# A two-layer streaming encoder step: the norms' squares added on VectorE, an empty memory left out, and the memory's closing spread over eight banks and two queues

## The chip, the cores and the metric

The kernel runs on one core of a Trainium2 chip. Its time is the device time of the whole program in microseconds (us). The core has five engines that run at once: TensorE (PE, matrix products into the PSUM memory, which has eight banks), VectorE (DVE), ScalarE (ACT), GpSimd (POOL) and SyncE (SP, which starts transfers). Each has its own list of instructions and they meet through semaphores alone.

## What is computed

One inference step of a trunk of two layers, for a prompt of 1024 frames and for 8 running streams of 16 frames. Each layer is a token mixer (layer 0 a diagonal state space with a gated output, layer 1 an mLSTM with a matrix memory) and then a convolutional gated MLP, with an RMS norm before and after every sub-layer. Cut to what matters here:

```
def rms_norm(x, g):
    return x * rsqrt(mean(x * x) + eps) * g

out = ag[..., :D_MODEL] * sigmoid(ag[..., D_MODEL:])        # layer 0's gated output, ag = z @ w_glu
x = x + rms_norm(mix, g[1]); f = conv_ffn(rms_norm(x, g[2]))

# mLSTM, per chunk of the prompt and per head, memory C starts at zero
num = (q k^T * wts) v + a * (q C^T)
den = sum(q k^T * wts) + a * (q n)
C   = decay * C + (wg * v)^T k                                # C and n of the last chunk are outputs
```

## The kernel before

The 1152 frames (1024 of the prompt, 128 of the streams) are the columns of everything; D_MODEL lies in 8 tiles of 128 rows. Columns go in three blocks of 384.

**The gated projection with the first norms.** `front` runs 24 steps (3 blocks of columns by 8 tiles `m`). A step is two weight tiles, each 24 products on TensorE (`products`, L1686). A weight tile is loaded by SP, rounded by ScalarE (`Weights.round`, L836), its remainder is taken by VectorE (`Weights.subtract`, L840), and TensorE waits for both. There are two rooms for weights: a load waits until the remainder of the tile before in its room is taken, and rounding waits until TensorE has used that tile. From the second block on the norms of the block before are put between the steps. `norm1` (class `Norm`) has six groups `g`: for each block the norm of the mixer's output (`r` = 0) and that of the new residual (`r` = 1). A group has four squares of 128x768 (ScalarE, L1526, into three rooms `sq`), their sums over rows and tiles as products with a matrix of ones (TensorE, `sums`, L1536, into bank 6), a root (ScalarE), an inverse (VectorE), its spread to all rows (TensorE, L1560, bank 7) and the scaling (VectorE, L1589). Groups 0 to 3 lie inside the 24 steps: squares at `m` = 0 and 4, sums at `m` = 1 and 5. Groups 4 and 5 come after. GpSimd moves residuals between SBUF and DRAM and takes the remainders `x_rest` (L1565). The order on every engine is written out by hand.

**The prompt cell.** `mlstm_prompt` goes over 8 chunks of 128 frames by 4 heads: two chunks unrolled, a loop, two unrolled. For a head TensorE makes the numerators in one bank pair: the scores by the values (`sc` by `v`, L2797) and then the queries by the memory `ct` (L2799, 4 tiles by 2 halves, added onto the same bank). It then projects the next head (L2666 to L2670), makes the key products (L2813) with the next scores between, and turns the output (L2821). VectorE forms the denominators (L2915 on), the normed row, four memory updates (L2937) and the gain. The third key product waits for the first update. GpSimd has cleared the memory before the first chunk.

**The closing.** A block of its own after the cell. TensorE turns the memory's 16 blocks by the key weights, 4 products each, into banks 0 to 3 in turn (L2966). ScalarE copies each to one of 8 rooms (L2981), SP stores it, 256 KB (L2990). Then the four rows of `n` go through banks 4 to 7 (L2971, L2984, L2993). SP waits for all stores, then a barrier, and `mlstm_down` begins with its weight loads and a clearing of `f`.

## Time and profile before

| | us |
|---|---|
| three runs | 3810.05, 3814.1, 3818.66 |
| median | 3814.1 |
| profiled execution, its time | 3816.18 |
| its span, first to last instruction | 3814.2 |
| TensorE busy in it | 3430.0 (90%) |
| VectorE, ScalarE, GpSimd busy | 1939.5 (51%), 1119.3 (29%), 482.8 (13%) |
| mean granted clock of TensorE | 0.943 of full speed |

A row of the timeline gives start, duration, engine, line, what is written from what, and in brackets how long the engine had been idle and whose work ended that. One product of 32-bit numbers stands as two records. Matmuls overlap, so the distance between two starts is what one costs. Rows of DMA queues name the engine that started the transfer with a q behind it.

### The profile page before, as it was taken

What the parts mean: (1) busy time and instruction counts of PE and PEld (TensorE: products, weight loads), DVE (VectorE), ACT (ScalarE), POOL (GpSimd) and SP (SyncE); (2) the same over time, 40 slices, a digit from 0 to 9 for tenths busy, and PEclk for the clock granted to TensorE, in tenths of its full rate; (3) what the DMA queues carried; (4) which work ended last, traced back from release to release, by engine and by line L of the source; (5) the groups of instructions that cost most, each with busy time, mean ns of one, the idle gap of its engine ahead of it and who ended that gap; (6) DMA issues with size and microseconds to landing.
All of it is one profiled execution on the core that took longest, in us unless ns stands there. A gap on an engine that the chain in (4) does not pass through costs nothing. (4 is left out here: it accounts for less than half of the span.)

```text
span 3814.2 us, 54162 instructions
## 1 busy us (share of the span) xinstructions
PE 3430.0 (90%) x20489; PEld 3239.3 (85%) x20489; DVE 1939.5 (51%) x2954; ACT 1119.3 (29%) x1816; POOL 482.8 (13%) x721
## 2 busy tenths in 40 slices
PE   5549999999999999999759799979959999999997
PEld 4439989999999998999546688879959999999996
DVE  7933455444544464222434466646554555555555
ACT  5233343233223333222223122221133222232221
POOL 2240111010001021000110322310001000000000
PEclk7669999999999999999879899989979999999998
DMA  3445431111111133223256322221033344344433
GB/s 80 133 128 139 130 103 45 45 40 45 43 41 40 45 111 106 105 102 108 57 203 257 89 78 77 78 72 39 31 115 118 123 131 131 116 128 128 127 115 109
DMA packets 357406, 372.72 MB, mean 98 GB/s; under 512 B 42696, under 2 KB 293832, under 8 KB 357060
## 3 DMA queue, kind: packets, MB, share of 16 engines
q1 hardware_dynamic: 340262, 330.43, 27.7%
q0 software_dynamic: 9760, 31.95, 2.7%
q10 hardware_dynamic: 7176, 7.35, 0.6%
q8 instruction: 157, 2.57, 0.3%
q14 instruction: 51, 0.42, 0.0%
HBM read 264.68 MB, written 102.63 MB: 96 GB/s over the span
## 5 line engine op out<-in xcount | busy, mean ns | idle before, releaser
L1686 PE MATMUL pair<-x_head,w_head 128*128 128x384 f32 x1488 | 505.1, 339 | 52.3 <-DVE w_rest L840 28.4
L1686 PE MATMUL pair<-x_rest,w_head 128*128 128x384 f32 x1488 | 501.6, 337 | 0.0
L1686 PE MATMUL pair<-x_head,w_rest 128*128 128x384 f32 x1488 | 501.5, 337 | 0.0
L840 DVE TENSOR_TENSOR w_rest<-w_raw,w_head 128x1024 fp32r<-128x1024 f32 x228 | 291.5, 1279 | 412.8 <-ACT w_head L836 412.7
L836 ACT ACTIVATE w_head<-w_raw 128x1024 fp32r<-128x1024 f32 x228 | 242.2, 1062 | 690.5 <-PE pair L856 167.1
L1336 PE MATMUL pair<-x_head,w_head 128*128 128x384 f32 x1056 | 358.4, 339 | 8.7 <-DVE w_rest L840 7.4
L1336 PE MATMUL pair<-x_head,w_rest 128*128 128x384 f32 x1056 | 353.8, 335 | 0.0
L1336 PE MATMUL pair<-x_rest,w_head 128*128 128x384 f32 x1056 | 353.7, 335 | 0.0
L1686 PEld LDWEIGHTS pair<-x_head,w_head 128*128 128x128 f32 x1488 | 283.1, 190 | 57.5 <-issue 48.2
L1429 DVE SCALAR_TENSOR_TENSOR cv<-u,par,cv 128x1024 f32<-128x1024 f32 x88 | 112.8, 1282 | 341.8 <-ACT u L1395 341.8
L1954 DVE SCALAR_TENSOR_TENSOR cv<-u,par,cv 128x1024 f32<-128x1024 f32 x88 | 112.8, 1281 | 340.9 <-ACT u L1895 340.9
L1686 PEld LDWEIGHTS pair<-x_rest,w_head 128*128 128x128 f32 x1488 | 283.1, 190 | 0.0
L1686 PEld LDWEIGHTS pair<-x_head,w_rest 128*128 128x128 f32 x1488 | 282.6, 190 | 0.0
L1336 PEld LDWEIGHTS pair<-x_head,w_head 128*128 128x128 f32 x1056 | 198.7, 188 | 24.5 <-issue 20.2
L1336 PEld LDWEIGHTS pair<-x_rest,w_head 128*128 128x128 f32 x1056 | 198.8, 188 | 0.0
L1336 PEld LDWEIGHTS pair<-x_head,w_rest 128*128 128x128 f32 x1056 | 198.8, 188 | 0.0
L1390 ACT ACTIVATE cv<-pair,par 128x384 f32<-128x384 f32 x132 | 88.5, 670 | 335.9 <-PE pair L1336 335.9
L1358 PE MATMUL pair<-a_head,w_head 128*128 128x384 f32 x528 | 180.8, 342 | 1.7 <-DVE f L1457 1.5
L1856 PE MATMUL pair<-a_head,w_head 128*128 128x384 f32 x528 | 179.9, 341 | 2.2 <-DVE f L1985 1.0
L1856 PE MATMUL pair<-a_head,w_rest 128*128 128x384 f32 x528 | 177.6, 336 | 0.0
L1856 PE MATMUL pair<-a_rest,w_head 128*128 128x384 f32 x528 | 177.6, 336 | 0.0
L1358 PE MATMUL pair<-a_head,w_rest 128*128 128x384 f32 x528 | 177.5, 336 | 0.0
(514 smaller groups left out, 6869.4 us busy)
## 6 DMA issues: line engine op xcount, KB each, us to landing
w_raw<-in_ffn_w_up_dram SPq DMA_DIRECT2D x88, 512.0 KB, 3.9
hs<-in_state_mlstm_C_dram SPq DMA_DIRECT2D x32, 1024.0 KB, 8.1
c_room<-in_state_mlstm_C_dram SPq DMA_DIRECT2D x64, 512.0 KB, 5.7
out_dram<-c_room SPq DMA_DIRECT2D x64, 512.0 KB, 4.6
w_raw<-in_s_w_glu_dram SPq DMA_DIRECT2D x48, 512.0 KB, 3.9
w_raw<-in_ffn_w_down_dram SPq DMA_DIRECT2D x44, 512.0 KB, 3.7
w_raw<-in_mlstm_w_up_dram SPq DMA_DIRECT2D x32, 512.0 KB, 4.2
xm_d<-xm SPq DMA_DIRECT2D x16, 576.0 KB, 3.9
```

What stands on the lines that cost most here:

```text
L836: act.activation(self.head[slot][:, :], self.raw[slot][:, :], ACT.Copy).then_inc(self.rounded, 1)
L840: dve.tensor_tensor(self.rest[slot][:, :], self.raw[slot][:, :], self.head[slot][:, :].bitcast(F32), ALU.subtract).then_inc(self.split, 1)
L1336: m = pe.matmul(banks[k % 2][c][:, 0:TB], lhs[k % 2][:, P * i:P * i + P], rhs[:, i, TB * c:TB * c + TB], start=(i == 0 and q == 0), stop=( ...
L1358: ins = pe.matmul(banks[m % 2][c][:, 0:TB], lhs[m // 4][:, cols], rhs[s][:, k, TB * c:TB * c + TB], start=(k == 0 and q == 0), stop=(k == ...
L1390: act.activation(cv[g][:, TB * c:TB * c + TB], bk[c][:, 0:TB], ACT.Identity, scale=at(par, t, TAP + H, TAP + H + 1), bias=at(par, t, BIAS, ...
L1429: ins = dve.scalar_tensor_tensor(out=cp, in0=up[:, j:j + SEQ], scalar=tw, in1=cp, op0=ALU.mult, op1=ALU.add)
L1686: m = pe.matmul(out[:, 0:TB], lhs[slot][:, P * k:P * k + P], rhs[:, k, TB * c:TB * c + TB], start=(k == 0 and q == 0), stop=(k == KD - 1 a ...
L1856: ins = pe.matmul(out[:, 0:TB], lhs[m // 4][:, cols], rhs[s][:, k, TB * c:TB * c + TB], start=(k == 0 and q == 0), stop=(k == 1 and q == 2))
L1954: ins = dve.scalar_tensor_tensor(out=cp, in0=up[:, j:j + SEQ], scalar=tw, in1=cp, op0=ALU.mult, op1=ALU.add)
```

## The change

Three edits that do not touch one another. First, for groups 0 to 3 of `norm1` VectorE adds the four squares into the first one's room (`gather`, three additions), and TensorE multiplies that one alone by the ones. ScalarE makes all four squares at `m` = 0 and 4; the second and the fourth share a room, so the fourth square waits for the first addition. Second, in the prompt's first chunk the numerators are closed after the scores by the values, since the memory is zero there. Third, the closing goes through banks 0 to 7; even blocks are copied by ScalarE and stored by SP, odd ones are copied by VectorE and stored by GpSimd's queue. The rows of `n` now wait for the copies of the last four blocks.

```diff
...
-    def __init__(self, env, f, x_dram, post, pre, h_head, h_rest, x, sq, wide, small):
+    def __init__(self, env, f, x_dram, post, pre, h_head, h_rest, x, sq, wide, small, gathers=0):
...
+        self.gathered, self.gathers = sem("gathered"), gathers
...
-            if n >= 3:
-                act.wait_ge(self.summed, n - 2)
+            if g < self.gathers:
+                if g and k == 0:
+                    act.wait_ge(self.gathered, 3 * g)
+                if g and k == 2:
+                    act.wait_ge(self.summed, g)
+                if k == 3:
+                    act.wait_ge(self.gathered, 3 * g + 1)
+            elif n >= 3:
+                if self.gathers:
+                    act.wait_ge(self.gathered, 3 * min(g, self.gathers))
+                act.wait_ge(self.summed, self.sums_of(g, k - 3) + 1)
...
-            act.activation(self.sq[n % 3][:, :, :], src, ACT.Square).then_inc(self.squared, 1)
+            act.activation(self.slot(g, k)[:, :, :], src, ACT.Square).then_inc(self.squared, 1)
+    def slot(self, g, k):
+        return self.sq[(g + (0, 1, 2, 1)[k]) % 3 if g < self.gathers else (self.HALF * g + k) % 3]
+    def sums_of(self, g, k):
+        if k < 0:
+            g, k = g - 1, k + self.HALF
+        return g if g < self.gathers else self.gathers + self.HALF * (g - self.gathers) + k
+    def gather(self, dve, g, k0, k1):
+        for k in range(k0, k1):
+            dve.wait_ge(self.squared, self.HALF * g + k + 1)
+            if k > 1:
+                dve.wait_ge(self.gathered, 3 * g + k - 1)
+            dve.tensor_tensor(self.slot(g, 0)[:, :, :], self.slot(g, 0)[:, :, :], self.slot(g, k)[:, :, :], ALU.add).then_inc(self.gathered, 1)
...
     def sums(self, pe, g):
-        for k in range(self.HALF):
-            n = self.HALF * g + k
-            pe.wait_ge(self.squared, n + 1)
+        parts = (0,) if g < self.gathers else range(self.HALF)
+        for k in parts:
+            if g < self.gathers:
+                pe.wait_ge(self.gathered, 3 * g + 3)
+            else:
+                pe.wait_ge(self.squared, self.HALF * g + k + 1)
...
-                    m = pe.matmul(self.env.bank[6][:, P * j:P * j + P], self.sq[n % 3][:, h, P * j:P * j + P], self.env.ones[:, :],
-                                  start=(k == 0 and h == 0 and j == 0), stop=(k == self.HALF - 1 and h == 1), skip_group_check=True)
+                    m = pe.matmul(self.env.bank[6][:, P * j:P * j + P], self.slot(g, k)[:, h, P * j:P * j + P], self.env.ones[:, :],
+                                  start=(k == 0 and h == 0 and j == 0), stop=(k == parts[-1] and h == 1), skip_group_check=True)
...
     def roots(self, act, g):
-        act.wait_ge(self.summed, self.HALF * g + self.HALF)
+        act.wait_ge(self.summed, self.sums_of(g, 0 if g < self.gathers else self.HALF - 1) + 1)
...
-                 wides(A0 + 33792), small)
+                 wides(A0 + 33792), small, 4)
...
                 glu.scalar(act, k)
...
-                        norm1.squares(act, g + m // 4, 2 * h, h + 2, glu.free, KD * (c - 1))
-                    if c and m in (1, 5) and h == 1:
-                        norm1.squares(act, g + m // 4, 3, 4, glu.free, KD * (c - 1))
+                        norm1.squares(act, g + m // 4, 2 * h, 2 * h + 2, glu.free, KD * (c - 1))
...
                 c, m = k // KD, k % KD
...
+                if c and m in (1, 5):
+                    norm1.gather(dve, g + m // 4, 2, 4)
                 w.subtract(dve, 2 * k + 2, 0)
+                if c and m in (0, 4):
+                    norm1.gather(dve, g + m // 4, 1, 2)
...
-                    for t in range(-1, HT):
+                    empty = isinstance(c, int) and c == 0
+                    for t in range(-1, 0 if empty else HT):
...
-                                pe.matmul(half(n, k), cell.sc[y][:, :], cut_half(cell.v[y], k), start=True, stop=False)
+                                ins = pe.matmul(half(n, k), cell.sc[y][:, :], cut_half(cell.v[y], k), start=True, stop=empty)
...
-            t_c, e_c, s_n = env.sem("t_c"), env.sem("e_c"), env.sem("s_n")
+            t_c, s_n = env.sem("t_c"), env.sem("s_n")
+            kept_c = [env.sem(f"kept_c{k}") for k in range(2)]
...
+            BLOCKS = HEADS * HT
+            def keep(eng, p):
+                for n in range(p, BLOCKS, 2):
+                    eng.wait_ge(t_c, n + 1)
+                    if n >= R:
+                        eng.wait_ge(s_c[n % R], 16 * (n // R))
+                    if p == 0:
+                        ins = eng.activation(out[n % R], bank[n % 8][:, :], ACT.Copy)
+                    else:
+                        ins = eng.tensor_copy(out[n % R], bank[n % 8][:, :])
+                    ins.then_inc(kept_c[p], 1)
+            def store(eng, p):
+                for n in range(p, BLOCKS, 2):
+                    eng.wait_ge(kept_c[p], n // 2 + 1)
+                    eng.dma_start(c_out[0, 0, n // HT, P * (n % HT):P * (n % HT) + P, :], out[n % R]).then_inc(s_c[n % R], 16)
...
                 @block.tensor
                 def _(pe):
                     for h in range(HEADS):
...
-                            if n >= 4:
-                                pe.wait_ge(e_c, n - 3)
+                            if n >= 8:
+                                pe.wait_ge(kept_c[n % 2], (n - 8) // 2 + 1)
...
-                                ins = pe.matmul(bank[n % 4][:, P * k:P * k + P], ct[h][:, k, P * v:P * v + P], cell.bd[:, 1, HT * h + k, :],
+                                ins = pe.matmul(bank[n % 8][:, P * k:P * k + P], ct[h][:, k, P * v:P * v + P], cell.bd[:, 1, HT * h + k, :],
...
                     for h in range(HEADS):
+                        pe.wait_ge(kept_c[h % 2], (BLOCKS - 4 + h) // 2 + 1)
...
                 @block.scalar
                 def _(act):
-                    for n in range(HEADS * HT):
-                        act.wait_ge(t_c, n + 1)
-                        if n >= R:
-                            act.wait_ge(s_c[n % R], 16 * (n // R))
-                        act.activation(out[n % R], bank[n % 4][:, :], ACT.Copy).then_inc(e_c, 1)
+                    keep(act, 0)
                     for h in range(HEADS):
-                        act.wait_ge(t_c, HEADS * HT + h + 1)
-                        act.activation(nrow[h], bank[4 + h][0:1, :], ACT.Copy).then_inc(e_c, 1)
+                        act.wait_ge(t_c, BLOCKS + h + 1)
+                        act.activation(nrow[h], bank[4 + h][0:1, :], ACT.Copy).then_inc(kept_c[0], 1)
+                @block.vector
+                def _(dve):
+                    keep(dve, 1)
+                @block.gpsimd
+                def _(pool):
+                    store(pool, 1)
...
                 @block.sync
                 def _(sp):
-                    for n in range(HEADS * HT):
-                        sp.wait_ge(e_c, n + 1)
-                        sp.dma_start(c_out[0, 0, n // HT, P * (n % HT):P * (n % HT) + P, :], out[n % R]).then_inc(s_c[n % R], 16)
+                    store(sp, 0)
                     for h in range(HEADS):
-                        sp.wait_ge(e_c, HEADS * HT + h + 1)
+                        sp.wait_ge(kept_c[0], BLOCKS // 2 + h + 1)
...
-                        sp.wait_ge(s_c[k], 16 * (HEADS * HT // R))
+                        sp.wait_ge(s_c[k], 16 * (BLOCKS // R))
...
```

## Rows read from the trace of the kernel before

**Rows 1.** The page, part 1: busy us, share of the span, instructions.
```profile
PE 3430.0 (90%) x20489; PEld 3239.3 (85%) x20489; DVE 1939.5 (51%) x2954; ACT 1119.3 (29%) x1816; POOL 482.8 (13%) x721
```

**Rows 2.** Windows: stretch, length, busy PE, PEld, DVE, ACT, POOL, PEclk, DMA, GB/s.
```profile
340.00:560.00 220.00, 208.60 (x1277) 206.19 (x1276) 105.24 (x128) 82.37 (x101) 30.46 (x33) 0.97 0.42 129
...
2134.00:2138.00 4.00, 4.00 (x26) 3.63 (x25) 0.72 (x4) 0.38 (x1) 0.00 (x0) 1.00 0.00 1
```

**Rows 3.** Groups by form from 290 to 560 us.
```profile
L836 ACT ACTIVATE w_head<-w_raw 128x1024 fp32r<-128x1024 f32 x47 | 49.6, 1054 | 43.7 <-PE pair L1686 39.1 <-DMA w_raw<-in_s_w_glu_dram 4.7
...
L1536 PE MATMUL pair<-ones,sq 128*128 128x128 f32 x288 | 33.1, 275 | 0.0
...
L1526 ACT ACTIVATE sq<-f 128x768 f32<-128x768 f32 x12 | 9.6, 835 | 13.6 <-PE pair L1536 13.6
...
L1585 DVE TENSOR_TENSOR x_even<-x_even,f 128x768 f32<-128x768 f32 x8 | 7.4, 949 | 0.0
```

**Rows 4.** Timeline of TensorE around one group of squares.
```profile
400.48 0.41 PE L1686 MATMUL pair<-x_head,w_head 128*128 128x384 f32 x1 [0.35 <-issue]
...
413.07 5.52 PE L1536 MATMUL pair<-ones,sq 128*128 128x128 f32 x48
...
418.35 0.42 PE L1686 MATMUL pair<-x_head,w_head 128*128 128x384 f32 x1
```

**Rows 5.** Timeline of VectorE beside the first squares of group 1.
```profile
403.10 1.23 DVE L840 TENSOR_TENSOR w_rest<-w_raw,w_head 128x1024 fp32r<-128x1024 f32 x1 [2.25 <-ACT w_head L836]
...
406.10 1.22 DVE L840 TENSOR_TENSOR w_rest<-w_raw,w_head 128x1024 fp32r<-128x1024 f32 x1 [1.77 <-ACT w_head L836]
```

**Rows 6.** Timeline of VectorE and of GpSimd at 443 us.
```profile
443.44 7.44 DVE L840 TENSOR_TENSOR w_rest<-w_raw,w_head 128x1024 fp32r<-128x1024 f32 x1 [1.83 <-ACT w_head L836]
...
442.64 7.15 POOL L1565 TENSOR_TENSOR x_rest<-f,x_head 128x768 fp32r<-128x768 f32 x4
```

**Rows 7.** Timeline of TensorE and of ScalarE after it.
```profile
450.98 0.66 PE L1686 MATMUL pair<-x_head,w_head 128*128 128x384 f32 x1 [5.34 <-issue]
...
456.95 0.49 ACT L1720 ACTIVATE gate<-pair 128x384 f32<-128x384 f32 x1 [9.69 <-PE pair L1686]
```

**Rows 8.** Timeline of TensorE in the first chunk of the prompt cell.
```profile
2153.50 2.00 PE L2813 MATMUL pair<-p_v,p_kw 128*128 128x256 f32 x8
...
2156.64 3.64 PE L2799 MATMUL pair<-f,p_qa 128*128 128x256 f32 x16
...
2160.12 1.05 PE L2666 MATMUL pair<-p_xc,bd 128*128 128x128 f32 x8
```

**Rows 9.** Timeline of VectorE in the same steps.
```profile
2148.65 0.22 DVE L2915 TENSOR_SCALAR p_small<-pair,cols 128x1 f32<-128x1 f32 x1 [2.70 <-PE pair L2799]
...
2151.49 0.69 DVE L2897 TENSOR_TENSOR p_qa<-p_q,p_row 128x512 f32<-128x512 f32 x1 [0.28 <-ACT p_q L2834]
...
2154.67 0.75 DVE L2937 SCALAR_TENSOR_TENSOR f<-f,p_row,pair 128x513 f32<-128x513 f32 x1 [0.57 <-PE pair L2813]
...
2160.32 0.22 DVE L2915 TENSOR_SCALAR p_small<-pair,cols 128x1 f32<-128x1 f32 x1 [2.70 <-PE pair L2799]
```

**Rows 10.** Timeline of the closing: TensorE, ScalarE, then SP's queue.
```profile
2514.19 17.00 PE L2966 MATMUL pair<-bd,f 128*128 128x128 f32 x128 [3.15 <-PEq L2752]
...
2531.22 0.60 ACT L2981 ACTIVATE p_h<-pair 128x512 f32<-128x512 f32 x1 [0.30 <-PE pair L2966]
...
2534.80 0.59 ACT L2984 ACTIVATE p_xc<-pair 1x512 f32<-1x512 f32 x1 [0.29 <-PE pair L2971]
...
2538.54 0.93 SPq L826 DMA_DIRECT2D w_raw<-in_mlstm_w_down_dram  x2
```

**Rows 11.** A copy out of PSUM by group; transfers: KB, median us to landing.
```profile
L1017 DVE COPY rows<-pair 128x512 f32<-128x512 f32 x9 | 6.2, 691 | 10.5 <-PE pair L982 10.5
...
x_res<-x_even POOLq DMA_DIRECT2D x8, 384.0 KB, 4.4
...
y_odd<-x_res POOLq DMA_DIRECT2D x4, 384.0 KB, 8.4
```

## The prediction

> **What bounds the kernel now.** I read the page first. TensorE is busy for 90% of the span and VectorE for 51% [rows 1]. TensorE is the engine that sets the pace in most of the program, so work taken off it is worth its own time only where TensorE has no other wait in that place. The change touches three places, and each was read in its own stretch. The stage windows [rows 2] show the first: between 340 and 560 us, where the gated projection runs with the first norms between its tiles, TensorE is busy 208.6 of 220 us at a granted clock of 0.97. The second is the first chunk of the prompt cell, from 2125 us on, where TensorE is at full clock and busy without a break once its data are there (the stretch from 2134 us is one such). The third is the closing of that cell, some 24 us long.
>
> The timeline of each stretch then says which wait ends last. In the projection TensorE goes from the tile products to the sums of squares and back without a gap [rows 4]. ScalarE rounds each weight tile, VectorE subtracts, and only then may TensorE use it. In the prompt cell TensorE runs its steps back to back and VectorE waits 2.70 us in each for the numerators [rows 8, 9]. In the closing TensorE is back to back as well, and ScalarE waits for it 0.3 us before each copy [rows 10].
>
> **Part A, squares added on VectorE.** For groups 0 to 3 the 24 products with `ones` become 6. One group of 24 (48 records) holds TensorE from 413.07 to 418.35, 5.28 us [rows 4]. A quarter is 1.32 us, so 3.96 us go in each group. Four groups give 15.8 us. Groups 4 and 5 keep their products (288 records are 6 groups of 48 [rows 3]).
>
> What is added: three additions of 128x768 in each group, 12 in all, at 0.95 us each by the same operation on the same shape [rows 3], 11.4 us on VectorE. They are free if they stay under the tile products, so the question is who waits behind them. The second and third additions stand before a subtraction in the next step. By then VectorE has more than 2 us to spare, and TensorE needs the sum only after two more tiles. The first addition is the tight one. It stands on VectorE between two subtractions, ScalarE's fourth square waits for it, and behind that square the rounding of the next weight tile is queued, then VectorE's subtraction, then TensorE. In the group at 400 us: the subtraction is 403.10 to 404.33, the addition would end at 405.2, the square (0.83 [rows 3]) at 406.1, the rounding (1.06) at 407.1, the subtraction (1.23) at 408.3. Before, that subtraction ended at 407.33 [rows 5]. TensorE runs three tiles from 400.48 to 413.07 [rows 4], 4.2 us each, so it asks for the third at 408.9: 0.5 us to spare. In groups 0 and 3, whose rows repeat this pattern, the same walk leaves 0.2 and 0.5 us.
>
> Group 2 falls into another stretch: GpSimd makes four `x_rest` subtractions from 442.64 to 449.79, and VectorE's subtraction, started at 443.44, lasts 7.44 us instead of 1.23 [rows 6]. TensorE stands 5.34 us and comes back at 450.98 [rows 7]. The addition goes behind this: 451.8, square 452.7, rounding 453.8, subtraction 455.0. TensorE comes back at the lower of its clock levels, its first tile is done only at 456.95 instead of 455.2 [rows 7], so this one is covered by nearly 2 us. I take 0.2 us off for small misses: A is -15.6. Bounds: -15.8 at best. At worst each first addition is late by its whole 0.95 us, -12.0.
>
> **Part B, no memory products in the first chunk.** Eight products per head (16 records) hold TensorE from 2156.64 to 2160.12, 3.48 us, in a step of 11.67 us (2148.65 to 2160.32) [rows 8, 9]. Four heads make 13.9 us, the upper bound. Without them a step of TensorE alone is 8.19 us. VectorE now takes over part of the bound. It starts 0.20 us after TensorE leaves the products (2148.65, and 2160.12 less a step) and ends its last operation 2.70 us before its next start at 2160.32, at 2157.6: 8.96 us, of which 0.28 and 0.57 are waits that shrink when it is late [rows 9]. TensorE without the products offers the next numerators after 8.39 us, VectorE is free after 9.16, so from the second head on VectorE is 0.7 us late. That lateness passes to TensorE once: the third key product waits for the first memory update. It is at 5.05 us after the step's start (2153.50) and would be at about 5.5. So steps two to four are 8.2, 8.6 and 8.7 us, and the step into the second chunk, which has its products again, pays back 0.5. Sum: 3.48 + 3.48 + 3.07 + 2.97 - 0.5 = 12.5 us. From 2134 us on no transfer runs [rows 2], so the data of all four heads have landed by the time the shorter first head is through. The worst bound: VectorE keeps all its inner waits and is behind by its 0.7 us as well, 9.66 us a step: 3.48 + 3 x 2.0 - 0.7 = 8.8.
>
> VectorE's two-input operations lie nearer to GpSimd's in this tighter step, and [rows 6] show what one such meeting can cost. The Trainium skill, "SBUF — State Buffer", section "Who interferes with whom", says that a VectorE instruction with two SBUF inputs and a GpSimd instruction that reads SBUF exclude each other for the whole instruction. By that rule the sum would lose up to about one GpSimd operation a head. The query product, one such operation, takes 0.69 us in every step before, as in this row [rows 9]; the trace has no tighter step to look at, so I leave the loss to a rival.
>
> **Part C, the closing.** Sixteen blocks are turned by TensorE in one piece of 17.00 us. In the steady part ScalarE copies a block in 0.60 us and waits 0.30 for TensorE before it, so blocks are 0.9 us apart; the four rows follow, and before the last of them too ScalarE waits for TensorE [rows 10]. So neither the fourth bank nor ScalarE holds anybody: eight banks and a second copier remove a wait that does not exist. The new waits of the row products on banks 4 to 7 are on copies that end at least two products earlier. The end of the stage hangs on the row path, which stays on ScalarE and SP: last copy from 2534.80, then SP's store, then the barrier, and the next stage starts at 2538.54. The last odd block goes another way: VectorE's copy 0.69 us (a 128x512 copy out of PSUM), GpSimd's issue 0.72, landing 4.4 us for a store of 384 KB [rows 11]: 2531.2 + 0.7 + 0.7 + 4.4 = 2537.0, still inside. C is 0. Bounds: -0.3, and +3.4 if the landing takes the 8.4 us of GpSimd's slowest group of transfers [rows 11].
>
> **The sum.** -15.6 - 12.5 + 0 = -28.1 us. The profiled execution took 3816.2 us (span 3814.2), so 3788.1 us of its own. It lies 2.1 us above the median of the runs, 3814.1; on the median's footing the prediction is 3786.0 us.
>
> **Rivals.**
> - *VectorE or GpSimd bounds the first chunk harder than I walked through.* For: VectorE is full in the short step. Against: only three steps feel it. B becomes -8.8, the time 3790.
> - *The first additions push the weight tiles late.* For: 0.2 and 0.5 us to spare, and the chain goes over three engines. Against: even a whole addition too late gives -12.0 instead of -15.6; with a stall as well behind the group at 443 us, -9. The time is 3790 to 3793.
> - *The closing gets slower,* because GpSimd's stores land after the rows. For: its transfers land in 4.4 to 8.4 us [rows 11]. Against: 1.5 us of cover. +1 to +3.4, so 3787 to 3789.
> - *The change does not do what it says:* TensorE's time goes but its place is a wait of the same size (weight loads that are late by the 4 us that the sums used to give them). For: some roundings do wait for a transfer, 4.7 us in all. Against: their waits for TensorE come to 39.1 us [rows 3]. Then A is 0 and the whole is -12.5: 3801.6.
> - *Slower than before.* Mechanism: at each of the four first additions TensorE stands long enough that its clock falls to the lower level. After the wait of 5.34 us the next tile took 456.95 - 450.98 = 6.0 us instead of 4.2 (1.8 lost) [rows 7]. To be slower by over 0.2% (7.6 us, about what a measurement of this kernel can tell from no change) the four must cost 28.1 + 7.6 = 35.7 us, 8.9 each, so a stand of 7.1 us at each. Only the held subtraction at 443 us comes near that (7.44 [rows 6]), once. Should it decide, about 3823.
>
> **How the numbers follow.** My forecast 0.64 (own range 3781 to 3791). First chunk bound harder 0.10; weight tiles late 0.10; closing slower 0.07; A given back 0.04; slower 0.02; the rest, 0.03, is more than I count, for instance groups 4 and 5 or the stage after also gaining, down to 3778. Range: the forecast, less 3.3 for the bounds (15.8 + 13.9 + 0.3 against 28.1: 1.9) and the spread of medians (the three runs lie 4 us either side), gives 3779. Above it reaches the late-tile case with some of the spread, 3797. Faster by over 0.2% means below 3806.5: all but the slower case and part of those near the given-back case, 0.94; same 0.04; slower 0.02.
>
> **What would show it.** In the projection: groups of 12 records with `ones` where 48 stood, about 1.3 us long, four of them, and no new wait of TensorE right after the tile in which the first addition lies; the 5.34 us gap unchanged in size. In the first chunk: distances of about 8.2 to 8.7 us between heads and VectorE with no wait before the denominators. In the closing: TensorE still 17 us for the blocks, copies alternating between ScalarE and VectorE with each waiting over 1 us, the next stage starting the same 24 us after the first turn. The prediction is wrong if new idle time of TensorE shows up before a weight tile at four places, if steps in the first chunk are over 9.5 us, or if the closing's tail grows by more than 1 us.

## The result and the profile after

The changed kernel takes 3785.7 us (median of four runs, 3778.5 to 3792.5), the kernel before 3815.1 (four runs, 3810.1 to 3818.7): ratio 0.9924, interval 0.9902 to 0.9945. That is 29.4 us less between these medians, and 28.4 less than the three runs that stood before the prediction. Predicted were 28.1 us less and 3786.0 us. The profiled execution is the fastest of the four, 3778.51 us with a span of 3776.4. Between the two profiled spans lie 37.8 us, so more than the medians differ by: readings below go by stretches, not by spans.

The page, part 1, and two windows of after, as [rows 1] and [rows 2]:

```profile
PE 3388.8 (90%) x20281; PEld 3200.6 (85%) x20281; DVE 1957.3 (52%) x2974; ACT 1116.1 (30%) x1808; POOL 491.0 (13%) x729
```

```profile
340.00:560.00 220.00, 203.18 (x1193) 200.34 (x1192) 130.02 (x159) 95.58 (x123) 33.79 (x39) 0.97 0.42 128
2114.00:2118.00 4.00, 3.96 (x24) 3.43 (x24) 3.43 (x7) 0.37 (x1) 0.35 (x1) 1.00 0.00 0
```

TensorE has 208 records less: 144 of the squares' products (288 became 144 [rows 3]) and 64 of the first chunk. The second window lies in another part of a step than the one shown before [rows 2], so the two do not compare; over the first chunk's four steps VectorE is busy 29.1 of 35.5 us, before 27.4 of 46.7.

**The projection.** Groups by form from 290 to 560 us of after, answering [rows 3]:

```profile
L1567 PE MATMUL pair<-ones,sq 128*128 128x128 f32 x144 | 17.0, 275 | 0.0
...
L1554 DVE TENSOR_TENSOR sq<-sq,sq 128x768 f32<-128x768 f32 x12 | 11.4, 952 | 0.4
```

The twelve additions take the 0.95 us each that the row for `x_even` gave. The timeline of TensorE at the first group (group 0) and at group 2, then of VectorE at group 2, answering [rows 4], [rows 6] and [rows 7]:

```profile
372.55 1.50 PE L1567 MATMUL pair<-ones,sq 128*128 128x128 f32 x12
373.80 0.42 PE L1717 MATMUL pair<-x_head,w_head 128*128 128x384 f32 x1
...
442.35 0.66 PE L1717 MATMUL pair<-x_head,w_head 128*128 128x384 f32 x1 [5.33 <-issue]
...
453.13 1.50 PE L1567 MATMUL pair<-ones,sq 128*128 128x128 f32 x12
```

```profile
434.81 7.44 DVE L840 TENSOR_TENSOR w_rest<-w_raw,w_head 128x1024 fp32r<-128x1024 f32 x1 [1.83 <-ACT w_head L836]
442.17 0.95 DVE L1554 TENSOR_TENSOR sq<-sq,sq 128x768 f32<-128x768 f32 x1
444.97 1.23 DVE L840 TENSOR_TENSOR w_rest<-w_raw,w_head 128x1024 fp32r<-128x1024 f32 x1 [1.85 <-ACT w_head L836]
```

A group of sums holds TensorE for 373.80 - 372.55 = 1.25 us instead of 5.28 [rows 4], 4.03 less. TensorE's waits in the projection (0.35, 0.78, 5.33, 0.35 and 3.01 us) are those of before, the same in size, and no new one stands behind a first addition; the stand at group 2 is 5.33 us, before 5.34 [rows 7].

**The first chunk.** TensorE's numerators, the scores by the values, in timeline rows of after (the first two heads, and the first head of the second chunk):

```profile
2109.35 1.10 PE L2831 MATMUL pair<-p_v,p_sc 128*128 128x256 f32 x4 [0.49 <-issue]
...
2117.61 1.03 PE L2831 MATMUL pair<-p_v,p_sc 128*128 128x256 f32 x4
...
2144.87 1.03 PE L2831 MATMUL pair<-p_v,p_sc 128*128 128x256 f32 x4
```

The two heads between start at 2126.85 and 2135.63. The steps are 8.26, 9.24, 8.78 and 9.24 us, 35.52 in all. Before, the same four took 46.75 (starts at 2132.36 and 2179.11). Gain 11.2. What fills a step of 9.24 us is seen in the timelines of TensorE, VectorE and GpSimd in the second head, answering [rows 8] and [rows 9]:

```profile
2118.93 1.13 PE L2699 MATMUL pair<-p_xc,bd 128*128 128x128 f32 x8 [0.29 <-issue]
...
2124.58 2.00 PE L2847 MATMUL pair<-p_v,p_kw 128*128 128x256 f32 x8 [0.56 <-DVE f L2971]
```

```profile
2119.92 0.96 DVE L2925 TENSOR_SCALAR p_e<-p_row,cols 128x128 f32<-128x128 f32 x1
...
2123.19 0.67 DVE L2967 TENSOR_SCALAR p_h<-p_h,p_mv,p_small 128x512 f32<-128x512 f32 x1 [0.44 <-POOL p_small L2905]
...
2125.75 0.75 DVE L2971 SCALAR_TENSOR_TENSOR f<-f,p_row,pair 128x513 f32<-128x513 f32 x1 [0.57 <-PE pair L2847]
```

```profile
2119.53 1.27 POOL L2910 TENSOR_TENSOR hs<-p_t,p_sz 128x512 f32<-128x512 f32 x1 [5.18 <-DVE p_t L2981]
2120.76 1.05 POOL L2902 TENSOR_TENSOR p_xc<-p_xc,m_par 128x512 f32<-128x512 f32 x1
2122.08 1.08 POOL L2905 TENSOR_TENSOR p_small<-p_small,minus_half 128x1 f32<-128x1 f32 x1 [0.27 <-DVE p_small L2963]
```

From the second head on VectorE's 2.70 us of waiting before the denominators [rows 9] is gone; in the first head 1.24 us of it is left. Its exponents (L2925), 0.29 us long before and 0.27 in the first head of after, last 0.96 here: they start at 2119.92, while GpSimd's gate product runs from 2119.53 to 2120.80, and end just behind it. GpSimd's power, one number a row, takes 1.08 us instead of 0.54 because VectorE's query product runs from 2122.06 to 2122.75 (without that product it takes 0.54, below), and VectorE then waits 0.44 us for the power. The Trainium skill, "SBUF — State Buffer", section "Who interferes with whom", has both: a VectorE operation with two SBUF inputs shuts out a GpSimd one that reads SBUF, and `tensor_scalar` can enter a mode that does so too, with the loser blocked for the whole instruction. The trace agrees for the query product (0.54 us more for the power) and for the exponents (0.69 more than in the first head); in which mode the exponents ran no row shows.

The two do not cost the same. In the third head the exponents are held as well, but the power, which starts level with the query product (both at 2131.32), is not, and that step is 8.78 us instead of 9.24:

```profile
2129.15 0.97 DVE L2925 TENSOR_SCALAR p_e<-p_row,cols 128x128 f32<-128x128 f32 x1
```

```profile
2131.32 0.54 POOL L2905 TENSOR_TENSOR p_small<-p_small,minus_half 128x1 f32<-128x1 f32 x1 [0.27 <-DVE p_small L2963]
```

**The closing.** Timeline of after, answering [rows 10]: TensorE, ScalarE, VectorE, then SP's queue:

```profile
2478.92 15.95 PE L3021 MATMUL pair<-bd,f 128*128 128x128 f32 x128 [3.37 <-PEq L2785]
```

```profile
2494.01 0.60 ACT L3001 ACTIVATE p_h<-pair 128x512 f32<-128x512 f32 x1 [1.19 <-PE pair L3021]
...
2498.49 0.59 ACT L3036 ACTIVATE p_xc<-pair 1x512 f32<-1x512 f32 x1 [0.29 <-PE pair L3027]
```

```profile
2493.12 0.69 DVE L3003 COPY p_kw<-pair 128x512 f32<-128x512 f32 x1 [1.09 <-PE pair L3021]
```

```profile
2502.24 0.93 SPq L826 DMA_DIRECT2D w_raw<-in_mlstm_w_down_dram  x2
```

Both copiers wait over 1 us for TensorE, as forecast. The blocks take 15.95 us instead of 17.00, but blocks are 0.89 us apart in the steady part with either closing, and what varies is how long the first ones run at the lower clock: granted 0.50 for about 5 us before and about 3 us here. From the start of the last row copy to the next stage's load it is 2502.24 - 2498.49 = 3.75 us, before 2538.54 - 2534.80 = 3.74 [rows 10]. The transfers of the closing, by group: KB and median us to landing. GpSimd's queue takes 2.3 us where [rows 11] gave 4.4 and 8.4 for larger ones:

```profile
out_dram<-p_kw SPq DMA_DIRECT2D x2, 256.0 KB, 2.6
out_dram<-p_kw POOLq DMA_DIRECT2D x2, 256.0 KB, 2.3
```

### The profile page after: what moved, and what is told of

It is laid out like the page before. It is cut to its first block and busy times, and to the rows that moved or that the text cites. A ratio compares the mean times of both kernels' runs of the same rounds, so it can differ in the third digit from the quotient of the medians.

```text
span 3776.4 us, 53763 instructions
## 1 busy us (share of the span) xinstructions
PE 3388.8 (90%) x20281; PEld 3200.6 (85%) x20281; DVE 1957.3 (52%) x2974; ACT 1116.1 (30%) x1808; POOL 491.0 (13%) x729
```

## The experiments

### Each part alone

Each part of the diff was put into the kernel before by itself.

> The kernel before with part A alone (VectorE adds the squares of groups 0 to 3). My theory: TensorE loses 3.96 us of products in each of four groups and gives almost nothing back, so the distance from the first product with ones of group 0 to the first of group 3 shrinks from 127.7 us (373.12 to 500.83 before) by 11.2 to 11.9 us, the run is 15 to 16 us faster. Rival (weight tiles late behind the first addition): new idle time of TensorE of 0.5 to 1 us before a tile in each group, 11 to 12 us faster in all. Rival (given back to the weight stream): under 4 us faster.

> The kernel before with part B alone (no memory products in the first chunk). The trace of the changed kernel gives 8.26, 9.24, 8.78, 9.24 us for the four steps that were 11.67. My theory after it: the same steps here, 11.2 us off the way from the first numerators to those of the second chunk, and the run 11 us faster. Forecast on record: 12.5. Rival: the steps were long there for a reason outside the chunk, then 12.5 here.

> The kernel before with part C alone (eight banks, two copiers, two queues). My theory: nothing, TensorE's 16 blocks still 0.89 us apart once its clock is up, and from TensorE's last row product to the next stage's first load 3.8 us as before; the 1.05 us that the first trace shows less is the earlier rise of the clock, so it may or may not come. Rival (the banks and the second copier help): 16 blocks in 16 us or less with the clock at the same low stretch as before, and the run 1 us or more faster. Rival (GpSimd's stores end the stage): the tail over 4.5 us.

| kernel | median us, runs | ratio to before | interval |
|---|---|---|---|
| before | 3816.49 (16) | | |
| squares alone | 3798.73 (5) | 0.9949 | 0.9936 to 0.9963 |
| products alone | 3802.99 (6) | 0.9967 | 0.9955 to 0.9979 |
| closing alone | 3814.93 (11) | 0.9999 | 0.9990 to 1.0008 |

*Squares.* By the medians -17.8 us (by the ratio 19.5, its interval 14 to 24). The first and the last of the four groups of sums stand in the timeline of TensorE 116.48 us apart, as in after (372.55 to 489.03); before it was 127.71 (373.12 to 500.83). 11.2 us come out of three groups, where 3 x 4.03 = 12.1 were taken from TensorE. The missing 0.85 is in group 2: from the end of the stand to its sums it takes 453.13 - 442.35 = 10.78 us in after, 9.93 before (450.98 to 460.91). The last product at the slow spacing of about 0.32 us (0.17 at full clock) starts at 447.3 there, 4.9 us after the restart, before at 454.0, 3.0 us after it. TensorE makes no wait in that place, it is the clock. All but one of the versions with part A take 10.3 to 11.0 us here, the one with the doubled addition (below) 9.84, so the loss is not fixed to the part. The rival that A is given back to the weight tiles falls, and so does the one that the first additions push them late.

*Products.* By the medians -13.5 us (interval 8 to 17). The four steps of the first chunk are 8.80, 9.24, 9.24 and 8.80, 36.08 in all, 10.7 less than before; the steps are the size to compare with the forecast of 12.5. In three more versions below that leave the cell as changed (addition twice, group 4, half closing after) the four take 37.07, 36.52 and 36.63, so the part gives 9.7 to 11.2 us from one execution to another. Half of that spread is the first step: 8.26 us where the granted clock in its first 4 us is 1.00 (after), 8.80 to 9.12 where it is 0.78 to 0.86.

*Closing.* No change within 0.1%. From the first product of the blocks to the first of the rows it is 16.96 us, before it was 16.92:

```profile
2513.05 17.03 PE L2987 MATMUL pair<-bd,f 128*128 128x128 f32 x128 [3.15 <-PEq L2752]
2530.01 3.65 PE L2993 MATMUL pair<-bd,f 128*1 128x128 f32 x32
```

The tail is the same too: 3.75 us from the last row copy (2533.70) to the next load (2537.45). So the 15.95 us of after need not come from the edit: with the new closing and all its products seven executions took 15.9 (after) to 17.3 us (the version without queries, below), with the old one three took 16.7 (squares alone) to 17.3 (products alone). Three of the seven lie at 15.9 to 16.1 and none of the three; whether that is chance is open. The two that differ most, after and the version without queries, have the same closing, and differ in the time at the lower clock.

### How much room the first additions have

In the changed kernel VectorE does one more operation of 0.95 us just before each first addition.

```diff
             if k > 1:
                 dve.wait_ge(self.gathered, 3 * g + k - 1)
+            else:
+                dve.tensor_tensor(self.slot(g, 0)[:, :, :], self.slot(g, 0)[:, :, :], self.slot(g, 0)[:, :, :], ALU.max).then_inc(self.again, 1)
+                dve.wait_ge(self.again, g + 1)
```

> The changed kernel, and before each first addition VectorE makes one more operation of the same size (the maximum of the first square with itself, which changes nothing), 0.95 us and a wait more. It tests how much room the first addition has. My theory by the walk on record: 0.2 to 0.5 us of room in groups 0, 1 and 3, so TensorE stands 0.5 to 0.9 us before the second weight tile of each of those steps, and in group 2 nothing, since there are 2 us of cover. Rival (more room than I think, or the fourth square is not in the chain): no new wait of TensorE anywhere.

The time is 3790.72 us (one run). The timeline of TensorE shows a new stand in groups 0, 1 and 3 and none in group 2. That of group 1 is at 408.12 (0.33 in brackets); those of groups 0 and 3:

```profile
371.65 0.41 PE L1720 MATMUL pair<-x_head,w_head 128*128 128x384 f32 x1 [0.54 <-issue]
```

```profile
487.67 0.34 PE L1720 MATMUL pair<-x_head,w_rest 128*128 128x384 f32 x1
488.31 0.41 PE L1720 MATMUL pair<-x_head,w_head 128*128 128x384 f32 x1 [0.30 <-issue]
```

The bracket counts from the modelled end of the product before, 0.34 us after its start, while products start 0.17 us apart. By the starts the delays are 371.65 - 370.77 - 0.17 = 0.71 us in group 0, 0.50 in group 1 (407.45 to 408.12) and 488.31 - 487.67 - 0.17 = 0.47 in group 3. The added operation and its step cost 0.99 us (402.99 to 403.98 in VectorE's timeline), so the room was some 0.3, 0.5 and 0.5 us: the 0.2, 0.5 and 0.5 of the walk. The path is the one that was walked, and in the kernel as changed it just holds.

### A fifth group

Group 4's squares are added on VectorE too (`norm1` with 5 instead of 4).

```diff
             w.subtract(dve, 2 * steps + 1, 1)
+            norm1.gather(dve, 4, 1, 4)
             norm1.inverse(dve, 4)
```

> The changed kernel with the squares of group 4 added on VectorE as well, just after the 24 steps. My theory: the additions stand behind VectorE's subtraction that GpSimd's four x_rest products hold until 520 us (8.2 us for 1.2), so the sum of group 4 is ready only at 524 instead of 520.4 us; TensorE saves 4 us of products and waits for longer than that, so the way from the first tile after the 24 steps to the products of the next stage gets 2 to 4 us longer. Rival (TensorE's products bound this place too): 4 us shorter.

The time is 3794.07 us (one run). The place, in the timelines of VectorE, GpSimd and TensorE:

```profile
513.66 8.21 DVE L840 TENSOR_TENSOR w_rest<-w_raw,w_head 128x1024 fp32r<-128x1024 f32 x1 [1.09 <-ACT w_head L836]
521.79 3.07 DVE L1554 TENSOR_TENSOR sq<-sq,sq 128x768 f32<-128x768 f32 x3
```

```profile
513.62 7.15 POOL L1596 TENSOR_TENSOR x_rest<-f,x_head 128x768 fp32r<-128x768 f32 x4
```

```profile
524.91 2.50 PE L1567 MATMUL pair<-ones,sq 128*128 128x128 f32 x10 [7.84 <-DVE sq L1554]
```

The additions stand behind a subtraction that GpSimd's four operations hold for 8.21 us, and here no tile product is left to cover them: TensorE stands 7.84 us and starts again at the lower clock. From the restart after the stand of 3 us to the stand of 4.20 us behind group 5 it takes 40.13 us (512.67 to 552.80), in after 34.56. That is 5.6 us lost, more than I expected, by the same edit that gained 4 us a group elsewhere.

### What holds the first chunk's steps

In the changed kernel the first chunk's query product, whose result nobody reads there, is left out.

```diff
                     ge(dve, numbered, c, h, 1, -1)
+                    if isinstance(c, int) and c == 0:
+                        dve.sem_inc(aqd, 1)
+                        return
                     dve.tensor_tensor(cell.qa[y][:, :, :], cell.q[y][:, :, :], bcast(cell.row[h][:, P:2 * P], 1, HT),
```

> The changed kernel, and in the first chunk VectorE leaves out the product of the queries with the decay, which nobody reads there. Same outputs. My theory: VectorE bounds steps two to four of the first chunk and each loses 0.69 us of it, and with it the meeting of that product with GpSimd's power (GpSimd 1.08 instead of 0.54 us, VectorE waiting 0.44 for it); steps of 8.3 to 8.6 us instead of 8.8 to 9.2, 2 us less in all. Rival (GpSimd's chain bounds the step: gate product, skip product, power): steps unchanged within 0.2 us. Rival (TensorE waits for VectorE's gain product alone): shorter steps but TensorE's wait of 0.3 us before the projection stays.

The time is 3787.71 us (5 runs), ratio 0.9928, interval 0.9914 to 0.9941: not to be told from the changed kernel. The steps are 8.03, 8.71, 8.70 and 9.24, in all 34.68, 0.84 less than in after, where 2 were expected. VectorE's rows in the second head show why:

```profile
2123.25 0.97 DVE L2925 TENSOR_SCALAR p_e<-p_row,cols 128x128 f32<-128x128 f32 x1
...
2125.99 0.67 DVE L2970 TENSOR_SCALAR p_h<-p_h,p_mv,p_small 128x512 f32<-128x512 f32 x1 [0.66 <-POOL p_small L2905]
```

The power is back at 0.54 us, but VectorE comes to the normed row sooner and waits for it 0.66 us. The exponents are still held by GpSimd's gate product. The step is 8.7 us with the power free and the exponents held, as the third of after; the last step, whose query product belongs to the second chunk and stays, has the power at 1.07 us and is 9.24 long. So the gate product was cut down as well, with the query product back (first chunk only; its gated output is left out, and `hs` is cleared there ahead of the steps, which the cut below does not show):

```diff
                     ge(pool, joined2, c, h, 1, 1)
+                    if isinstance(c, int) and c == 0:
+                        pool.tensor_tensor(hs[:, HT * h, 0:8], cell.t1[y][:, 0, 0:8], cell.sz[h][:, 0, 0:8],
+                                           ALU.mult).then_inc(finished, 1)
+                        return
```

> The changed kernel, but in the first chunk GpSimd's product with the gate is cut from 128x512 to 128x8, and hs is cleared there once ahead of the steps; so the first chunk's gated output is left out. It takes away the GpSimd operation that lies over VectorE's exponents in the short step. My theory (the two exclude each other): VectorE's exponents back from 0.96 to 0.27 to 0.30 us in all four steps, GpSimd's power no longer late, steps of 8.2 to 8.6 us. Rival (VectorE's exponents are long for another reason): 0.96 stays.

The time is 3786.37 us (one run), the steps are 8.27, 8.73, 8.72 and 8.73. The timelines of GpSimd and of VectorE:

```profile
2123.73 0.21 POOL L2913 TENSOR_TENSOR hs<-p_t,p_sz 128x8 f32<-128x8 f32 x1 [5.19 <-DVE p_t L2987]
2123.89 1.05 POOL L2904 TENSOR_TENSOR p_xc<-p_xc,m_par 128x512 f32<-128x512 f32 x1
```

```profile
2124.12 0.90 DVE L2931 TENSOR_SCALAR p_e<-p_row,cols 128x128 f32<-128x128 f32 x1
```

The exponents are as long as ever: GpSimd's next operation, the skip product, has moved into the gap and holds them instead. They end at 2125.02, just behind its 2124.94. The power is at 0.54 us in all four steps, and that is where the step got shorter. The third try keeps all products of GpSimd, leaves out the query product as before, and only orders GpSimd's list in the first chunk anew: power and mask first, then the skip product, and the gate product after VectorE's next exponents.

```diff
+                    if isinstance(c, int) and c == 0:
+                        ge(pool, aimed, c, h, 1, 1)
+                        pool.tensor_tensor(cell.small[y][:, 2:3], cell.small[y][:, 3:4], env.minus_half[:, :], ALU.pow).then_inc(powed, 1)
+                        mask(*after(c, h))
...
+                        ge(pool, joined2, c, h, 1, 1)
+                        ge(pool, exp_in, c, h, 1, 3)
+                        pool.tensor_tensor(hs[:, tiles, cut(c)], cell.t1[y][:, :, :], cell.sz[h][:, :, :],
+                                           ALU.mult).then_inc(finished, 1)
+                        return
```

> The kernel of e4 (no query product in the first chunk), and in the first chunk GpSimd takes its work in another order: power, mask, skip product, and the gate product last and only after VectorE's next exponents. Same outputs. In e8 the exponents stayed at 0.90 us because the skip product moved into the place of the gate product. My theory: VectorE's exponents and GpSimd's two-input products exclude each other, so with none of them there the exponents take 0.27 to 0.30 us, no operation of VectorE waits for the power for more than 0.2 us, and steps two to four are 8.2 to 8.5 us. Rival (the exponents are long because of ScalarE's or TensorE's access at that time): 0.9 us stays. The run 26 to 32 us under the kernel before.

3786.53 us (5 runs), ratio 0.9923, interval 0.9909 to 0.9936, again the changed kernel's. In VectorE's timeline:

```profile
2126.28 0.29 DVE L2937 TENSOR_SCALAR p_e<-p_row,cols 128x128 f32<-128x128 f32 x1
...
2128.95 0.67 DVE L2982 TENSOR_SCALAR p_h<-p_h,p_mv,p_small 128x512 f32<-128x512 f32 x1 [0.66 <-POOL p_small L2903]
```

The exponents are free at last, 0.29 us, and the steps are 8.67, 8.63, 8.64 and 8.73 (the first one at a granted clock of 0.84 in its first 4 us). The second and third are 0.07 us shorter than with the exponents held (8.71 and 8.70 in the version without queries), so 0.67 us more of VectorE cost next to nothing there, and the step after the four is 12.44 where it was 11.67. The 8.2 to 8.5 us and the wait of under 0.2 that I expected did not come: with nothing held, the step still is 8.6 us, made of waits between engines (0.52 for ScalarE's copy of the row, 0.66 for the power, 0.57 for TensorE's key products). It is a loop of results, not a full engine.

### Whether the closing's new banks and copier could do anything

In both kernels a block of the closing gets 2 of its 4 products, so that TensorE offers blocks twice as often; half of each stored block is left out.

```diff
-                            for k in range(HT):
+                            for k in range(HT // 2):
```

> The kernel before, but the closing makes only two of the four products of each of the 16 blocks, so half of each stored block of C is left out (it stores what the bank held). My theory: TensorE sets the pace of the closing at full work, so with half of it the next in line shows: ScalarE's copy of 0.60 us and its wait on the same engine; blocks 0.6 to 0.7 us apart instead of 0.89. Rival (SP's transfers or another thing bounds it already): still near 0.89.

> The changed kernel with the same halved products in the closing. My theory: now eight banks and two copiers do help, blocks follow TensorE at about 0.45 to 0.5 us, unless the stores (256 KB in 2.3 to 2.8 us, eight rooms) bound them at 0.7 us, which is 256 KB at the 360 to 390 GB/s that the densest slices show. Rival (two copiers never help): as far apart as in the halved kernel before.

One run each: 3815.41 and 3784.56 us (the kernel before beside them 3812.37). ScalarE alone in the first, ScalarE and VectorE in the second:

```profile
2525.25 1.13 ACT L2981 ACTIVATE p_qa<-pair 128x512 f32<-128x512 f32 x2
```

```profile
2496.76 0.60 ACT L3001 ACTIVATE p_qa<-pair 128x512 f32<-128x512 f32 x1 [0.30 <-PE pair L3021]
...
2497.21 0.69 DVE L3003 COPY p_qa<-pair 128x512 f32<-128x512 f32 x1 [0.20 <-PE pair L3021]
```

With half the products and the old closing ScalarE copies without a wait, two blocks each 0.96 us (2524.30, 2525.25, 2526.21), so one alone is the bound at 0.48 us a block, not the 0.6 to 0.7 that I expected from the duration of one copy: its copies, 0.60 us each, start 0.48 us apart. With the new one blocks leave every 0.45 us and both copiers still wait for TensorE. So the edit takes the bound off ScalarE only once TensorE offers blocks twice as fast as it does, and even then it is worth 0.03 us a block. The whole closing, to the next stage's load, is 17.8 us in the first (2518.27 to 2536.07) and 18.6 in the second (2488.69 to 2507.24), but the two do not compare: the granted clock was low for about 4 us in the first and for 6 in the second. Two windows of the second, at its start and at full clock:

```profile
2488.70:2494.70 6.00, 6.00 (x28) 6.00 (x29) 1.89 (x3) 1.79 (x3) 1.23 (x2) 0.50 0.38 139
2494.70:2498.70 4.00, 4.00 (x38) 4.00 (x37) 2.85 (x5) 2.54 (x5) 2.12 (x4) 0.99 0.93 351
```

For the first 6 us the granted clock is 0.50, and after them the transfers run at 351 GB/s with the 16 DMA engines busy for 93%. That the stores would be the next bound is argued from that share; no run took them away.

## Why the prediction was right

The time and the sum are right to 0.3 and 1.3 us. In part that is luck: the four runs of the changed kernel lie 14 us apart, the interval of the ratio spans 21 to 37 us, and two of the terms were off with opposite signs.

*Part A, forecast 15.6, by stretches 16.5 to 18.1.* The mechanism is shown: the sums cost 1.25 us, the additions 0.95, no new wait, and the room of the first addition is there and is as small as walked. Of 4 x 4.03 = 16.1 us, group 2 gives back 0.85, against the 0.2 that I had taken off. What no step foresaw is a gain from the clock behind group 3. TensorE stands 3.01 us there in every version. Timeline and windows of the kernel before, then of the squares alone, then of after:

```profile
526.68 0.66 PE L1686 MATMUL pair<-x_head,w_head 128*128 128x384 f32 x1 [3.01 <-DVE f L1726]
```

```profile
525.70:529.70 4.00, 3.02 (x9) 3.05 (x10) 2.70 (x3) 3.86 (x5) 2.79 (x3) 0.53 0.57 187
529.70:533.70 4.00, 4.00 (x16) 4.00 (x16) 4.00 (x1) 0.14 (x1) 4.00 (x3) 0.61 0.00 0
```

```profile
512.00:514.00 2.00, 2.00 (x10) 2.00 (x9) 2.00 (x1) 2.00 (x3) 2.00 (x2) 0.60 0.53 197
514.00:516.00 2.00, 2.00 (x8) 2.00 (x7) 2.00 (x1) 0.10 (x1) 2.00 (x2) 0.54 0.00 0
```

```profile
510.80:514.80 4.00, 3.93 (x23) 3.96 (x24) 2.94 (x1) 3.23 (x5) 3.71 (x3) 1.00 0.33 118
```

Over all versions that have this stretch unchanged it goes by whether they have part A, and then in two kinds (us; the first column is the stretch from the start of group 0's sums to the stand of 4.20 us behind group 5, the second from the restart after the 3 us stand to group 4's sums):

| version | whole stretch | after the stand |
|---|---|---|
| before; closing alone; products alone; half closing before | 190.95; 190.79; 190.68; 190.67 | 7.06; 7.01; 6.97; 6.95 |
| squares alone; addition twice; narrow gate; half closing after | 174.45; 174.54; 174.27; 173.98 | 5.81; 5.72; 5.83; 5.80 |
| after; no queries; GpSimd's order | 172.88; 173.08; 172.95 | 4.24; 4.24; 4.24 |

The tile behind the stand takes 7.0 us in each execution without part A and 4.2 or 5.8 with it. So 16.1 - 0.85 + (7.06 - 4.24) = 18.1 is the 190.95 - 172.88 measured in after. Each number is one execution. That the clock falls for longer in the versions before is shown; why the shorter groups of sums ahead of the stand change it is not. The versions at 4.24 and at 5.8 hold the same instructions in this stretch, but for the doubled addition.

*Part B, forecast 12.5, measured 11.2 (10.7 alone, 9.7 at the least).* The mechanism is shown: TensorE's 3.48 us a head go and a step of other engines takes over part of the bound. The term that was mis-sized is the steps two to four, put at 8.2, 8.6 and 8.7 us and measured at 9.24, 8.78 and 9.24, 1.8 more in all; the step into the second chunk paid nothing back, where 0.5 was taken off (its start lies 11.66 us before the next, as any step of before). The walk let every operation keep its duration, and two did not: the exponents 0.29 to 0.96, the power 0.54 to 1.08 with 0.44 of waiting behind it. This is the mechanism that I had left to a rival of -8.8, and it is true in kind: the trace shows the exclusion. It is smaller in size, and the power alone carries it: a step is 9.24 us with both held (in the five versions with this cell, but for one of 9.47), 8.70 to 8.80 with the power free, 8.63 to 8.73 with both free (GpSimd's order). So the power costs some 0.5 us a step, 0.9 of the 1.8, and the exponents under 0.1. The rest is the walk's own: it let VectorE's lateness grow from 8.2 over 8.6 to 8.7 us, while the loop is at 8.6 from the second head on with nothing held. The wait of 0.3 us before each projection, which no version removed, is also part of it. By the code it is for VectorE's gain product (L2977), which reads the bank that the projection writes and ends at 2118.72, 0.2 us ahead of it; this was not tried.

*Part C, forecast 0, measured 0.* Shown alone, ratio 0.9999 with an interval of 0.9990 to 1.0008 (3.8 us faster to 3.1 slower), and with the blocks as far apart as forecast. The feared landing of 4.4 to 8.4 us on GpSimd's queue was 2.3 to 2.6.

*The signs cancel.* By stretches the parts give 18.1 + 11.2 = 29.3 us in after, against 28.1. The rest of the 37.8 us between the two profiled spans lies where the change took nothing away: 4.4 us between the stand behind group 5 and the prompt cell, 1.0 in the rest of the cell, 1.0 in the closing, 1.5 behind it and 0.6 ahead of group 0. The medians do not show it.

*Sums and readings of the forecast that do not hold.* The upper bound of +3.4 for part C does not come out of its row: 2531.2 + 0.7 + 0.7 + 8.4 = 2541.0 is 2.5 us behind 2538.54. The lower end of the range, 3779, is 7 us under the forecast, where the working names 1.9 (or 3.3) and 4. That no transfer runs from 2134 us on is true of the 4 us of the window only; over the four steps before, the DMA share is 0.22. Nothing in the result hangs on these.

*The rivals.* Weight tiles late, the change given back, closing slower and slower than before: all fall, the first two by the squares alone and the doubled addition, the third by the closing alone, the last because TensorE makes no new stand at a first addition. Its clock did change, but behind the two old stands: lower for longer in group 2 and for less behind group 3.

## What to carry to other kernels

A product with a matrix of ones is TensorE time that an idle VectorE can cut to a quarter, as long as a tile of other products covers the chain behind the added operation; walk that chain over all engines, because the same edit that gained 4 us a group cost 5.6 where no product covered it. When work goes off the bounding engine, ask which two operations of VectorE and GpSimd will now overlap that did not before, and then which of them somebody waits for: an operation of 0.29 us became one of 0.96 and cost under 0.1 us a step, a power of 0.54 us became one of 1.08 and cost 0.5. Taking one of GpSimd's operations away can put the next in the same place. More banks and a second copier do nothing while every copy already waits for TensorE, and a wait of 0.3 us before each copy is enough to see that.

## What the runs showed that was not expected

- A stand of TensorE of 3.01 us cost nothing more in three executions, 1.5 to 1.6 us in four and 2.8 us in the four without part A, with the same work behind it. The granted clock is 1.00 throughout in after; in the squares alone it is 0.60 and 0.54 in two windows of 2 us that begin 1 us behind the restart and 1.00 after them; in the kernel before 0.53 and 0.61 in two windows of 4 us. After the stand of 5.3 us the slow spacing lasted 3.0 us before and with the doubled addition, and 4.9 in after. What such a stand costs can't be read off one trace.
- An operation of VectorE with a single SBUF tensor, 128x128 of 32 bits, was held by GpSimd's product until that ended (0.29 to 0.96 us; 0.29 again once no GpSimd operation lay there). One of 128x1024 with two SBUF tensors lasted through four GpSimd operations in a row and ended 1.1 us behind the last of them (7.44 and 8.21 us instead of 1.23); no run took those away.
- Stores of 256 KB out of GpSimd's queue landed in 2.3 to 2.6 us beside 2.4 to 2.7 out of SP's in after, 2.6 to 3.1 beside 2.5 to 3.2 with the closing alone, while VectorE was copying out of PSUM.
